# Five changes of order in a two-block transformer kernel: where a residual is scaled, when weight strips are split, when rows are turned, and how heads end

## The chip, the cores and the metric

The kernel runs on one core of one Trainium2 chip. Times are device microseconds (us) of one execution. The kernel before takes 3137.26 us, the median of 3 runs (3134.35 to 3138.42). The core has a matrix engine (TensorE, PE in the profile, its weight loads PEld), three engines for elementwise work (VectorE is DVE, ScalarE is ACT, GpSimd is POOL), and a queue that issues the weight loads (SyncE, SP). The engines run their own instruction lists and wait for each other on semaphores.

## What is computed

The input is 512 tokens of 1024 features. Block 1 is a norm, a projection into a gated delta rule (4 heads) and a dilated window attention (4 heads of 128 in three groups), two gates and an output matrix. Block 2 has two layers, each of:

```python
x = x + 0.5 * swiglu(rms_norm_2(x, ffn1_norm[l]), ffn1_w_in[l], ffn1_w_out[l])
h = rms_norm_2(x, mix_norm[l])
z_mla, z_swa, z_na = jnp.split(h @ w_mix_in[l], [MLA_IN, MLA_IN + SWA_IN], axis=-1)
o = jnp.concatenate([rms_norm_2(o_mla, g[:MLA_OUT]), rms_norm_2(o_swa, ...), rms_norm_2(o_na, ...)], axis=-1)
x = x + o @ w_mix_out[l]
x = x + mem_xattn(rms_norm_2(x, mem_norm_x[l]), mem, mem_norm_m[l], ...)
x = x + 0.5 * swiglu(rms_norm_2(x, ffn2_norm[l]), ffn2_w_in[l], ffn2_w_out[l])
x = rms_norm_2(x, block_norm[l])
```

The mix has three attentions: latent attention (8 heads), windowed attention (4 heads of 64) and neighbourhood attention (4 heads of 64). The memory attention reads 256 memory tokens with 4 heads of 64. Every query and key head is normed (and some are rotated) before its scores. `swiglu` goes over 22 tiles of 128 hidden features.

## The kernel before

**Layout and precision.** Activations lie feature by token (`residual`, 8 tiles of 128x512). A matrix product in full precision is three matmuls: operands are split into a high part and a low part, and `halves_mm` (L378) issues high x high (L373), high x low and low x high (L374, L375). Weights come as strips of 128x1024 by DMA into a ring of four slots. ACT writes a strip's high part (`split_strip_act`, L358, cast at L361), DVE subtracts it from the strip and writes the low part (`split_strip_dve`, L364, L367). PE needs both, and there is room for two high parts, so the high part of strip s+2 waits until PE has finished strip s. A strip of 1024 columns is 24 matmuls on PE, each over 512 tokens.

**Feed-forward** (`ffn_pe` L405, `ffn_act` L473, `ffn_dve` L523). Per hidden tile PE multiplies two strips (gate, up). DVE scales each bank by the token's rstd (L536, L541), ACT takes the SiLU (L489), DVE multiplies (L547), ACT writes the product's high part (L494), DVE the low part (L549). Between these steps ACT and DVE split strips two ahead. The norm of the input is not applied in front of the matmuls: its sum over features is a matmul that `ffn_pe` issues after its third strip (`norm_pe`, L226), and rstd is used at the banks.

**Layer 2's first feed-forward.** The norm that ends layer 1 is folded into it. Squares are summed on GpSimd (L211, and the raw sum at L1766); PE sums both over the partitions (L226 and `raw_norm`, L1328); `folded_norm` on ACT (L1468) and DVE (L1615) makes a combined rstd out of the two in six short steps; then `normalise_residual` (L1625, instructions at L1627) scales the eight tiles of `residual` by layer 1's norm. `ffn_dve` calls it through `residual` after the first hidden tile.

**Jobs and units.** A *job* makes one pair of query or key heads or one head: matmuls of one strip, squares on ACT (L672), their sum over features on PE (L645, into a bank for sums), logarithm and exponential on ACT (L680, L683), gain or rstd on DVE (L710, L716), rotary steps on DVE (L733 to L738) and the product with the rstd (L748). A *unit* is 128 queries of one head: scores on PE (L833), bias and maximum on DVE (L962, L973), exponential on ACT (L903), turning on PE (L845), copy of the turned probabilities on ACT (L914), product with the values on PE (L859). Each engine has both as generators, and `take_turns` (L1013) runs them by one list of names that all three engines share: `mix_turns` (L1254) and `mem_turns` (L1260) in block 2, `sw_turns` (L2034) in block 1. A job j has two halves, "begin" (its matmuls and squares) and "finish" (the sum, rstd and products of job j-1). Normally begin j comes ahead of finish j-1; for numbers in `early` (`sums_first`, `sw_first`) finish comes ahead. Jobs that use split strips also split the strip two ahead, unless `split=False`.

**The mix's output** (L1376 to L1418). The eight feature tiles of the attention output are turned on PE (`rows_pe`); six inside the turns, the last two (which wait for the group norm's scaling, L1693) behind them; ACT and DVE write their halves (L1707 for the low one). `mix_out(n, ks)` (L1394) multiplies blocks ks of output tile n. Tiles 0 and 1 are multiplied first for blocks 0 to 5, then the memory's norm matmul and rows 6 and 7, then blocks 6 and 7 of both. DVE then scales the memory's eight tiles (L1721) ahead of the first residual addition (L1731) and the splits of strips 2 and on.

## Time and profile before

| | before |
|---|---|
| median of 3 runs | 3137.26 us (3134.35 to 3138.42) |
| the profiled execution | 3127.07 us |
| its span | 3125.2 us |
| PE busy | 2948.3 us (94%), 13424 matmuls |
| DVE, ACT, POOL busy | 1466.8, 1087.2, 237.8 us |
| mean granted clock of PE | 0.972 |
| share of PE in the chain that ended last | 65% |
| bytes read from memory | 234.51 MB, 76 GB/s over the span |

The profile is one execution, recorded instruction by instruction. A busy share says how much of the span an engine executed; a list of waits says for whom an engine stood idle just before an instruction; a timeline gives start and duration of each instruction or of a run of like ones, and in brackets the idle time before it with the instruction that ended it. The granted clock is the share of full speed that the chip's throttle gave to PE. A matmul's shown duration reaches to its modelled end and overlaps the next: consecutive matmuls start 0.23 us apart at full clock.

### The profile page before, as it was taken

What the parts mean: (1) busy time and instruction counts of PE and PEld (TensorE: products, weight loads), DVE (VectorE), ACT (ScalarE), POOL (GpSimd) and SP (SyncE); (2) the same over time, 40 slices, a digit from 0 to 9 for tenths busy, and PEclk for the clock granted to TensorE, in tenths of its full rate; (3) what the DMA queues carried; (4) which work ended last, traced back from release to release, by engine and by line L of the source; (5) the groups of instructions that cost most, each with busy time, mean ns of one, the idle gap of its engine ahead of it and who ended that gap; (6) DMA issues with size and microseconds to landing.
All of it is one profiled execution on the core that took longest, in us unless ns stands there. A gap on an engine that the chain in (4) does not pass through costs nothing.

```text
span 3125.2 us, 36179 instructions
## 1 busy us (share of the span) xinstructions
PE 2948.3 (94%) x13424; PEld 2326.3 (74%) x13424; DVE 1466.8 (47%) x2032; ACT 1087.2 (35%) x1771; POOL 237.8 (8%) x176
## 2 busy tenths in 40 slices
PE   8878989989899999998999999899999998999998
PEld 5567767768778888566768888788886677778886
DVE  5653247744354433555444443444434645354432
ACT  4412233433233222555333222322223645432221
POOL 0000000000010012100220002100022000120012
PEclk9989899989999999999999999999999999999999
DMA  3100121103322233011212232222322110223232
GB/s 119 54 14 14 64 81 54 51 31 95 124 78 97 98 102 139 23 50 34 71 56 90 100 105 94 71 99 94 105 93 101 34 48 31 71 81 100 94 109 73
DMA packets 68361, 238.04 MB, mean 76 GB/s; under 512 B 10272, under 2 KB 12448, under 8 KB 67616
## 3 DMA queue, kind: packets, MB, share of 16 engines
q1 hardware_dynamic: 66240, 227.87, 21.8%
q10 hardware_dynamic: 2016, 8.77, 0.8%
q8 instruction: 66, 1.08, 0.1%
q14 instruction: 39, 0.32, 0.0%
HBM read 234.51 MB, written 2.10 MB: 76 GB/s over the span
## 4 chain that ended last, share of the span: by engine, by line
PE 65%; DVE 3%; ACT 3%; issue 1%; DMA 0%; POOLq 0%; DVEq 0%; POOL 0%; ACTq 0%; SPq 0%; PEldq 0%
PE bank L373 18%; PE bank L374 18%; PE bank L375 18%; PE bank L859 2%; PE bank L833 2%; PE bank L635 2%; PE bank L845 1%; PE bank L645 1%; PE bank L1448 1%; ACT L_probs L903 1%; PE bank L1425 0%; DVE L_scores L951 0%; ACT L_w_hi L361 0%; DVE L_weight_ring_low L367 0%; PE bank L226 0%
## 5 line engine op out<-in xcount | busy, mean ns | idle before, releaser
L373 PE MATMUL bank<-L_h_hi,L_w_hi 128*128 128x512 f32 x1776 | 709.5, 400 | 32.1 <-DVE L_weight_ring_low L367 14.0
L374 PE MATMUL bank<-L_h_lo,L_w_hi 128*128 128x512 f32 x1776 | 695.0, 391 | 0.0
L375 PE MATMUL bank<-L_h_hi,L_weight_ring_low 128*128 128x512 f32 x1776 | 694.5, 391 | 0.0
L361 ACT CAST L_w_hi<-L_weight_ring 128x1024 fp32r<-128x1024 f32 (+2 forms) x292 | 325.7, 1115 | 923.0 <-PE bank L375 911.1
L367 DVE TENSOR_TENSOR L_weight_ring_low<-L_weight_ring,L_w_hi 128x1024 fp32r<-128x1024 f32 (+2 forms) x292 | 395.3, 1354 | 376.2 <-ACT L_w_hi L361 375.9
L373 PEld LDWEIGHTS bank<-L_h_hi,L_w_hi 128*128 128x128 f32 x1776 | 335.4, 189 | 116.4 <-issue 16.8
L374 PEld LDWEIGHTS bank<-L_h_lo,L_w_hi 128*128 128x128 f32 x1776 | 335.9, 189 | 74.7 <-issue 6.8
L375 PEld LDWEIGHTS bank<-L_h_hi,L_weight_ring_low 128*128 128x128 f32 x1776 | 335.7, 189 | 70.7
L373 PE MATMUL bank<-L_act_hi,L_w_hi 128*128 128x512 f32 x704 | 273.9, 389 | 0.0
L374 PE MATMUL bank<-L_act_lo,L_w_hi 128*128 128x512 f32 x704 | 273.9, 389 | 0.0
L375 PE MATMUL bank<-L_act_hi,L_weight_ring_low 128*128 128x512 f32 x704 | 273.9, 389 | 0.0
L373 PE MATMUL bank<-B_h_hi,B_w_hi 128*128 128x512 f32 x480 | 196.1, 409 | 4.9 <-ACT B_arena L2438 3.4
L211 POOL TENSOR_TENSOR L_squares_sum<-residual 128x512 f32<-128x512 f32 x9 | 11.2, 1243 | 2486.3 <-DVE residual L572 1008.5
L375 PE MATMUL bank<-B_h_hi,B_weight_ring_low 128*128 128x512 f32 x480 | 188.1, 392 | 0.0
L374 PE MATMUL bank<-h_low,B_w_hi 128*128 128x512 f32 x480 | 188.0, 392 | 0.0
L541 DVE TENSOR_TENSOR L_up<-bank,L_rstd 128x512 f32<-128x512 f32 x88 | 60.8, 690 | 243.8 <-PE bank L375 243.8
L859 PEld LDWEIGHTS bank<-L_area,L_probsT 128*128 128x128 f32 x960 | 131.5, 193 | 57.1 <-issue 25.6
L367 DVE TENSOR_TENSOR B_weight_ring_low<-B_weight_ring,B_w_hi 128x1024 fp32r<-128x1024 f32 (+1 forms) x94 | 106.4, 1133 | 142.9 <-ACT B_w_hi L361 140.4
L375 PEld LDWEIGHTS bank<-L_act_hi,L_weight_ring_low 128*128 128x128 f32 x704 | 132.2, 188 | 27.6
L374 PEld LDWEIGHTS bank<-L_act_lo,L_w_hi 128*128 128x128 f32 x704 | 132.2, 188 | 27.4
L373 PEld LDWEIGHTS bank<-L_act_hi,L_w_hi 128*128 128x128 f32 x704 | 132.2, 188 | 27.3
L361 ACT CAST B_w_hi<-B_weight_ring 128x1024 fp32r<-128x1024 f32 (+1 forms) x94 | 91.4, 974 | 154.7 <-PE bank L375 152.5
(304 smaller groups left out, 3901.6 us busy)
## 6 DMA issues: line engine op xcount, KB each, us to landing
L_weight_ring<-ffn_in SPq DMA_DIRECT2D x176, 512.0 KB, 3.2
L_weight_ring<-ffn_out SPq DMA_DIRECT2D x64, 704.0 KB, 4.0
B_weight_ring<-w_sqk SPq DMA_DIRECT2D x24, 512.0 KB, 3.2
B_weight_ring<-w_dn SPq DMA_DIRECT2D x16, 512.0 KB, 3.3
B_weight_ring<-w_gate SPq DMA_DIRECT2D x16, 512.0 KB, 3.2
L_weight_ring<-w_sna_qk SPq DMA_DIRECT2D x16, 512.0 KB, 3.2
L_weight_ring<-w_mix_out SPq DMA_DIRECT2D x16, 512.0 KB, 3.2
B_weight_ring<-w_sv SPq DMA_DIRECT2D x12, 512.0 KB, 3.3
```

The lines of the kernel that those rows point to most:

```text
L361: e.copy(hv.high(at)[:, 0:width], sh.ring[:, at % RING, 0:width]).then_inc(hv.w_hi_done, 1)
L367: e.tensor_tensor(hv.low(at)[:, 0:width], sh.ring[:, at % RING, 0:width], hv.high(at)[:, 0:width].bitcast(F32), ALU.subtract).then_inc(hv. ...
L373: e.matmul(out, a_hi, b_hi, start=start, stop=False)
L374: e.matmul(out, a_hi, b_lo, start=False, stop=False)
L375: return e.matmul(out, a_lo, b_hi, start=False, stop=stop)
L541: e.tensor_tensor(hv.up[:, :], sh.banks[2 * j + 1][:, :], sh.rstd[:, :], ALU.mult)\
L635: mm = e.matmul(bank[r0:r0 + rn, 0:job["width"]], w[:, off:off + rn], rhs, start=(i == 0 and m == 0), stop=(i == len(job["parts"]) - 1 and ...
L645: e.matmul(banks[sum_banks[b % len(sum_banks)]][:, 0:width], ones[0:kn, :], jb.sq[0:kn, b, 0:width], start=True, stop=True).then_inc(jb.su ...
L833: e.matmul(banks[b][:, 0:nk], q, k, start=True, stop=True).then_inc(at_.scored, 1)
L845: mm = e.transpose(banks[b][:, i * P:(i + 1) * P], at_.p[:, u % 2, kt * P:(kt + 1) * P], ident[:, :])
L859: mm = e.matmul(banks[at_.ob[ob]][:, c0:c0 + unit["dv"]], at_.pt[:, u % 2, i * P:(i + 1) * P], v, start=(i == 0), stop=(i == len(vs) - 1))
L903: e.activation(at_.p[:, u % 2, 0:nk], src, ACT.Exp, bias=at_.nm[:, s:s + 1], accum_out=at_.sums[:, s:s + 1]).then_inc(at_.exped, 1)
```

## The change

No instruction is added or removed on any engine; what changes is the order.

- `ffn_pe`: where a second norm matmul is wanted (layer 2's first feed-forward alone), both come after the second strip and not after the third. `ffn_dve`: the residual is scaled after the second hidden tile and not after the first.
- `sw_turns` and `sw_first`, block 1: job 6 is also one in which finish comes ahead of begin, and in the last of the four heads the turns end with job, job, unit, unit in place of job, unit, job, unit.
- The splits that ride on the eight jobs of the windowed and neighbourhood heads (and the last two latent ones) are taken out of the jobs and put between the two units of ten turns of `mix_turns`.
- The mix's output: tile 0's blocks 0 to 5, then rows 6 and 7 are turned, then tile 1's blocks 0 to 3, then the memory's norm matmul, then the remaining blocks.
- `mem_turns`: four jobs, three units, the last job, the rest; job 3 has finish ahead of begin.

```diff
@@ -419,7 +419,7 @@
                 mm.then_inc(sh.strip_done, 1)
-                if first and j == 1 and part == 0:
+                if first and (j, part) == ((1, 0) if more_norm is None else (0, 1)):
                     norm_pe(e, seen, sh)
@@ -550,9 +550,9 @@
     tile(0, 0, W_IN, split=False)
+    tile(1, 1, W_IN)
     if residual is not None:
         residual()
-    tile(1, 1, W_IN)
     with seen.loop(e, FT // 2 - 2, ready=[(sh.strip_done, 4), (sh.silu_done, 2), (hv.w_hi_done, 4),
@@ -1174,15 +1174,15 @@
                                      ones=(ones, QK2), scale=1.0 / QK2, gain=scaled_qg[:, layer, 0:1], rope="own", cos_sin=cs2,
-                                     dest=(qk[:, tile, :], QK2), split=h == MLA_HEADS - 1,
+                                     dest=(qk[:, tile, :], QK2), split=False,
                                      **({"needs": (v_done, layer * (2 * TT + 2) + TT + 1)} if h == 0 else {})))
...
                                      rows=(0, NOPE), width=T, ones=(ones, QK2), scale=1.0 / QK2, gain=g("mlak"),
-                                     dest=(qk[:, tile + 1, :], QK2), split=h == MLA_HEADS - 1))
+                                     dest=(qk[:, tile + 1, :], QK2), split=False))
 
...
             mem_parts = [[(k * P, (mem_hi[k], mem_lo[k])) for k in range(KT)]]
-            pair = dict(rows=(0, P), ones=(ones64, P), scale=1.0 / DH)
+            pair = dict(split=False, rows=(0, P), ones=(ones64, P), scale=1.0 / DH)
 
@@ -1195,9 +1195,10 @@
             mem_jobs = [dict(pair, parts=k_parts(1, KT, P, m_n, NMEM), width=NMEM, gain=g("memk"),
-                             dest=(qk[:, 2 * i + 1, :], P), split=i == 0) for i in range(2)]
+                             dest=(qk[:, 2 * i + 1, :], P)) for i in range(2)]
+            mem_jobs[0]["split"] = True
             mem_jobs[1]["needs"] = (v_done, (layer + 1) * (2 * TT + 2))
-            mem_jobs += [q_job(i, scaled_qg[:, layer, 3:4], mem_parts, number=jobs_before + len(mix_jobs) + 3 + i, split=False) for i in range(2)]
+            mem_jobs += [q_job(i, scaled_qg[:, layer, 3:4], mem_parts, number=jobs_before + len(mix_jobs) + 3 + i) for i in range(2)]
             mem_jobs[2]["needs"] = (sh.h_done, layer * H_PER + 3 * KT)
@@ -1253,11 +1254,12 @@
         for i in range(20):
-            mix_turns += ["unit", "unit"] + {17: ["norm"], 18: ["norm_used"]}.get(i, []) + ["job"]
+            mix_turns += ["unit"] + ["split"] * (i >= 10) + ["unit"] + {17: ["norm"], 18: ["norm_used"]}.get(i, []) + ["job"]
         mix_turns += ["unit", "unit", "row"] * 4
...
         mix_turns += ["unit"] * 2 + ["row"] + ["unit"] * 6
-        mem_turns = ["job"] * 5 + ["unit"] * (1 + 4 * TT)
+        mem_turns = ["job"] * 4 + ["unit"] * 3 + ["job"] + ["unit"] * (4 * TT - 2)
+        mem_first = (3,)
 
@@ -1400,16 +1402,18 @@
 
-                    for n in range(2):
-                        e.wait_ge(sh.x_done, seen.free(sh.x_done))
-                        halves_here(e, seen, sh, hv, at + n, True)
-                        mix_out(n, range(6))
+                    e.wait_ge(sh.x_done, seen.free(sh.x_done))
+                    halves_here(e, seen, sh, hv, at, True)
+                    mix_out(0, range(6))
+                    next(rows)
+                    next(rows)
+                    e.wait_ge(sh.x_done, seen.free(sh.x_done))
+                    halves_here(e, seen, sh, hv, at + 1, True)
+                    mix_out(1, range(4))
                     e.wait_ge(at_.o_done, 2 + 10 * layer + 8)
                     norm_pe(e, seen, sh, NMEM)
-                    next(rows)
-                    next(rows)
-                    for n in range(2):
-                        mix_out(n, range(6, KT))
+                    mix_out(0, range(6, KT))
+                    mix_out(1, range(4, KT))
                     for n in range(2, KT):
@@ -1429,7 +1433,7 @@
                     seen.ready(sh.h_done, KT)
-                    take_turns(mem_turns, job=jobs_pe_steps(e, seen, sh, jb, at, mem_jobs, hv, True),
+                    take_turns(mem_turns, job=jobs_pe_steps(e, seen, sh, jb, at, mem_jobs, hv, True, mem_first),
                                unit=attn_pe_steps(e, seen, sh, at_, mem_units, ident))
@@ -1546,6 +1550,11 @@
 
+                    def splits_act():
+                        for i in range(10):
+                            split_strip_act(e, seen, sh, hv, at0 + sna_at + i, KT * P)
+                            yield
+
                     def rows_act():
@@ -1561,7 +1570,7 @@
                     take_turns(mix_turns, job=jobs_act_steps(e, seen, sh, jb, mix_jobs, hv, at0 + sna_at - 2 * MLA_HEADS, sums_first),
-                               unit=attn_act_steps(e, seen, sh, at_, mix_units), norm=norms, row=rows)
+                               unit=attn_act_steps(e, seen, sh, at_, mix_units), norm=norms, row=rows, split=splits_act())
                     next(norms)
@@ -1579,7 +1588,7 @@
                     split_strip_act(e, seen, sh, hv, at0 + mem_q_at, KT * P)
-                    take_turns(mem_turns, job=jobs_act_steps(e, seen, sh, jb, mem_jobs, hv, at0 + mem_q_at - 1),
+                    take_turns(mem_turns, job=jobs_act_steps(e, seen, sh, jb, mem_jobs, hv, at0 + mem_q_at - 1, mem_first),
                                unit=attn_act_steps(e, seen, sh, at_, mem_units))
@@ -1695,6 +1704,11 @@
 
+                    def splits_dve():
+                        for i in range(10):
+                            split_strip_dve(e, seen, sh, hv, at0 + sna_at + i, KT * P)
+                            yield
+
                     def rows_dve():
@@ -1711,7 +1725,7 @@
                                unit=attn_dve_steps(e, seen, sh, at_, mix_units, stores("mix", o_tok, 8)),
-                               norm_used=scales, row=rows)
+                               norm_used=scales, row=rows, split=splits_dve())
                     next(scales)
@@ -1733,7 +1747,7 @@
                     seen.ready(sh.strip_done, 2)
-                    take_turns(mem_turns, job=jobs_dve_steps(e, seen, sh, jb, mem_jobs, hv, at0 + mem_q_at - 1, True),
+                    take_turns(mem_turns, job=jobs_dve_steps(e, seen, sh, jb, mem_jobs, hv, at0 + mem_q_at - 1, True, mem_first),
                                unit=attn_dve_steps(e, seen, sh, at_, mem_units, stores("mem", o_mem, 2)))
@@ -2032,8 +2046,9 @@
         sw_turns = ["job"] * 7 + ["unit"]
-        sw_turns += ["job", "job", "unit", "job", "job", "unit", "job", "unit", "job", "unit"] * (NH - 1) + ["unit"] * TT
-        sw_first = range(2 * len(sw_jobs) // NH, len(sw_jobs) + 1, len(sw_jobs) // NH)
+        sw_turns += ["job", "job", "unit", "job", "job", "unit", "job", "unit", "job", "unit"] * (NH - 2)
+        sw_turns += ["job", "job", "unit", "job", "job", "unit", "job", "job", "unit", "unit"] + ["unit"] * TT
+        sw_first = range(len(sw_jobs) // NH, len(sw_jobs) + 1, len(sw_jobs) // NH)
 
```

How this moves instructions, at three places. Behind a row's engine line stand the operation, the outputs and the inputs with the names of the program, and the shape.

DVE, layer 2's first feed-forward, from the norm's last step (L1622, in the changed kernel L1631) on, before:

```order
L1622 TENSOR_TENSOR L_rstd<-L_area 128x512
L536 TENSOR_TENSOR L_unsplit<-bank,L_rstd 128x512
L541 TENSOR_TENSOR L_up<-bank,L_rstd 128x512
L547 TENSOR_TENSOR L_unsplit<-L_up,L_unsplit 128x512
L549 TENSOR_TENSOR L_act_lo<-L_unsplit,L_act_hi 128x512
L1627 SCALAR_TENSOR_TENSOR residual<-residual,L_gains,L_area 128x512 x8
L536 TENSOR_TENSOR L_unsplit<-bank,L_rstd 128x512
L367 TENSOR_TENSOR L_weight_ring_low<-L_weight_ring,L_w_hi 128x1024
L541 TENSOR_TENSOR L_up<-bank,L_rstd 128x512
L367 TENSOR_TENSOR L_weight_ring_low<-L_weight_ring,L_w_hi 128x1024
L547 TENSOR_TENSOR L_unsplit<-L_up,L_unsplit 128x512
L549 TENSOR_TENSOR L_act_lo<-L_unsplit,L_act_hi 128x512
```

and after:

```order
L1631 TENSOR_TENSOR L_rstd<-L_area 128x512
L536 TENSOR_TENSOR L_unsplit<-bank,L_rstd 128x512
L541 TENSOR_TENSOR L_up<-bank,L_rstd 128x512
L547 TENSOR_TENSOR L_unsplit<-L_up,L_unsplit 128x512
L549 TENSOR_TENSOR L_act_lo<-L_unsplit,L_act_hi 128x512
L536 TENSOR_TENSOR L_unsplit<-bank,L_rstd 128x512
L367 TENSOR_TENSOR L_weight_ring_low<-L_weight_ring,L_w_hi 128x1024
L541 TENSOR_TENSOR L_up<-bank,L_rstd 128x512
L367 TENSOR_TENSOR L_weight_ring_low<-L_weight_ring,L_w_hi 128x1024
L547 TENSOR_TENSOR L_unsplit<-L_up,L_unsplit 128x512
L549 TENSOR_TENSOR L_act_lo<-L_unsplit,L_act_hi 128x512
L1636 SCALAR_TENSOR_TENSOR residual<-residual,L_gains,L_area 128x512 x8
```

The eight scalings of the residual move behind the four elementwise steps and two strip splits of the second tile.

DVE, the last head of block 1, the second-to-last job's product and what follows, before:

```order
L748 TENSOR_TENSOR B_arena<-B_gained,B_job_rstd 128x512
L962 TENSOR_TENSOR B_arena<-bank,B_arena 128x256
L962 TENSOR_TENSOR B_arena<-bank,B_arena 128x512 x2
L973 TENSOR_REDUCE B_neg_max<-B_arena 128x1
L733 TENSOR_TENSOR B_rope_tmp<-B_gained,B_arena 32x512
L734 TENSOR_TENSOR B_rope_tmp<-B_gained,B_arena 32x512
L736 TENSOR_TENSOR B_gained<-B_gained,B_arena 64x512
L738 TENSOR_TENSOR B_gained<-B_gained,B_rope_tmp 64x512
L748 TENSOR_TENSOR B_arena<-B_gained,B_job_rstd 128x512
```

and after:

```order
L748 TENSOR_TENSOR B_arena<-B_gained,B_job_rstd 128x512
L733 TENSOR_TENSOR B_rope_tmp<-B_gained,B_arena 32x512
L734 TENSOR_TENSOR B_rope_tmp<-B_gained,B_arena 32x512
L736 TENSOR_TENSOR B_gained<-B_gained,B_arena 64x512
L738 TENSOR_TENSOR B_gained<-B_gained,B_rope_tmp 64x512
L748 TENSOR_TENSOR B_arena<-B_gained,B_job_rstd 128x512
L962 TENSOR_TENSOR B_arena<-bank,B_arena 128x256
L962 TENSOR_TENSOR B_arena<-bank,B_arena 128x512 x2
L973 TENSOR_REDUCE B_neg_max<-B_arena 128x1
```

The rotary steps and the product of the last key move ahead of the three additions and the maximum of a unit.

ACT, one turn of the mix with the split in it, before (L361 casts the strip, L914 copies turned probabilities, L903 is a unit's exponential, L680 a job's logarithm):

```order
L672 ACTIVATE L_unsplit<-L_gained 128x512
L361 CAST L_w_hi<-L_weight_ring 128x1024
L914 COPY L_probsT<-bank 128x512
L903 ACTIVATE L_probs,L_row_sums<-L_scores,L_neg_max 128x256
L914 COPY L_probsT<-bank 128x512
L903 ACTIVATE L_probs,L_row_sums<-L_scores,L_neg_max 128x384
L680 ACTIVATE L_job_rstd<-bank 128x512
```

and after:

```order
L672 ACTIVATE L_unsplit<-L_gained 128x512
L914 COPY L_probsT<-bank 128x512
L903 ACTIVATE L_probs,L_row_sums<-L_scores,L_neg_max 128x256
L361 CAST L_w_hi<-L_weight_ring 128x1024
L914 COPY L_probsT<-bank 128x512
L903 ACTIVATE L_probs,L_row_sums<-L_scores,L_neg_max 128x384
L680 ACTIVATE L_job_rstd<-bank 128x512
```

The cast moves behind the first unit's copy and exponential; its low half on DVE moves in the same way behind a maximum.

## Rows read from the trace of the kernel before

**Rows 1.** The page's first part: engine, busy us (share of the span), instructions.

```profile
PE 2948.3 (94%) x13424; PEld 2326.3 (74%) x13424; DVE 1466.8 (47%) x2032; ACT 1087.2 (35%) x1771; POOL 237.8 (8%) x176
```

**Rows 2.** Waits of PE: line, waited for: us in total, times, longest.

```profile
PE bank L373 <- DVE L_weight_ring_low L367: 14.0, 4, 9.0
PE bank L833 <- DVE B_arena L748: 13.0, 4, 6.1
```

**Rows 3.** Timeline, layer 2's first feed-forward: start, duration, instruction, [idle before <-releaser].

```profile
1988.20 1.74 POOL L1766 TENSOR_TENSOR L_area<-L_area,L_squares 128x512 f32<-128x512 f32 x1
...
2009.78 5.38 DVE L1627 SCALAR_TENSOR_TENSOR residual<-residual,L_gains,L_area 128x512 f32<-128x512 f32 x8
...
2016.95 0.79 PE L373 MATMUL bank<-L_h_hi,L_w_hi 128*128 128x512 f32 x1 [9.04 <-DVE L_weight_ring_low L367]
```

**Rows 4.** Windows: us, busy of each engine (x), granted clock, DMA; and one wait.

```profile
1511.00:1515.00 4.00, 3.73 (x10) 2.66 (x9) 3.89 (x10) 1.46 (x2) 0.00 (x0) 0.58 0.21 63
1646.00:1650.00 4.00, 3.45 (x15) 2.84 (x16) 3.31 (x5) 1.58 (x3) 0.00 (x0) 1.00 0.37 131
2016.90:2020.30 3.40, 3.35 (x8) 2.67 (x9) 2.71 (x4) 1.08 (x2) 0.00 (x0) 0.51 0.00 0
...
1646.55 0.50 PE L373 MATMUL bank<-L_h_hi,L_w_hi 128*128 128x512 f32 x1 [1.65 <-DVE L_weight_ring_low L367]
```

**Rows 5.** Timeline, end of head 0 in block 1.

```profile
457.66 1.02 PE L645 MATMUL bank<-B_job_squares,shared_consts 128*128 128x512 f32 x2
...
459.93 0.63 ACT L683 ACTIVATE B_job_rstd<-B_job_rstd 128x512 f32<-128x512 f32 x1
...
463.55 0.69 DVE L748 TENSOR_TENSOR B_arena<-B_gained,B_job_rstd 128x512 f32<-128x512 f32 x1
...
467.03 0.68 DVE L733 TENSOR_TENSOR B_rope_tmp<-B_gained,B_arena 32x512 f32<-32x512 f32 x1
...
470.64 1.65 PE L833 MATMUL bank<-B_arena 128*128 128x128 f32 x6 [5.61 <-DVE B_arena L748]
```

**Rows 6.** Timeline, end of the last head in block 1.

```profile
632.24 1.49 DVE L973 TENSOR_REDUCE B_neg_max<-B_arena 128x1 f32<-128x1280 f32 x1
...
633.76 1.36 ACT L903 ACTIVATE B_arena<-B_arena,B_neg_max 128x1280 f32<-128x1280 f32 x1 [4.96 <-DVE B_neg_max L973]
...
637.95 1.06 PE L845 MATMUL bank<-shared_consts,B_arena 128*128 128x128 f32 x4
```

**Rows 7.** Timeline, turns of the mix in layer 1.

```profile
1410.01 1.03 ACT L361 CAST L_w_hi<-L_weight_ring 128x1024 fp32r<-128x1024 f32 x1
...
1411.58 1.10 PE L859 MATMUL bank<-L_area,L_probsT 128*128 128x64 f32 x8 [0.22 <-ACT L_probsT L914]
...
1419.16 0.69 DVE L710 TENSOR_TENSOR L_gained<-bank,L_rstd 128x512 f32<-128x512 f32 x1 [1.26 <-PE bank L375]
...
1443.54 1.12 PE L859 MATMUL bank<-L_area,L_probsT 128*128 128x64 f32 x4 [2.42 <-ACT L_probsT L914]
```

**Rows 8.** Timeline, the mix's output in layer 1.

```profile
1502.24 1.14 DVE L1693 TENSOR_SCALAR L_area<-L_area,L_group_sums 128x256 f32<-128x256 f32 x4 [2.25 <-ACT L_group_sums L1546]
...
1510.23 0.50 PE L373 MATMUL bank<-L_h_hi,L_w_hi 128*128 128x512 f32 x1 [1.72 <-DVE L_h_lo L1707]
...
1511.53 3.26 DVE L1721 SCALAR_TENSOR_TENSOR L_area<-L_memT,L_gains,L_job_rstd 128x256 f32<-128x256 f32 x8
...
1516.57 0.50 PE L373 MATMUL bank<-L_h_hi,L_w_hi 128*128 128x512 f32 x1 [1.20 <-DVE residual L1731]
```

**Rows 9.** Timeline, the memory queries in layer 1.

```profile
1569.94 0.59 PE L645 MATMUL bank<-L_unsplit,shared_consts 128*128 128x256 f32 x2
...
1571.96 0.42 ACT L683 ACTIVATE L_job_rstd<-L_job_rstd 128x256 f32<-128x256 f32 x1
...
1578.86 1.10 PE L645 MATMUL bank<-L_unsplit,shared_consts 128*128 128x512 f32 x2 [1.98 <-ACT L_job_rstd L683]
...
1583.98 0.69 PE L845 MATMUL bank<-shared_consts,L_probs 128*128 128x128 f32 x2 [1.52 <-ACT L_probs L903]
```

## The prediction, made before the changed kernel was run

> **What bounds the kernel now.** I read the page first. TensorE (PE) is busy for 94% of the span [rows 1], so only what PE executes or waits for can move the end; the change removes no matmul, so its whole room is the 177 us in which PE stands idle and the stretches in which it runs at half clock. Then I read the list of PE's waits, which says on whom it waits: two groups matter here, a split weight strip that comes late (14.0 us in 4 waits, one of them 9.0) and a query or key head that comes late in the first block (13.0 us in 4 waits) [rows 2]. Then the timelines of PE, VectorE (DVE) and ScalarE (ACT) around each edit, to see what ended last there. Last, the windows for the granted clock. I worked each edit forward from its first moved instruction with the durations of the rows; all times of the changed kernel below are such estimates.
>
> **Residual scaling and its norm, layer 2's first feed-forward.** Today PE stops for 9.04 us on the low half of a weight strip [rows 3]. DVE could not write it: it ran the eight scalings of the residual (5.38 us) first. Behind this stands the fold of the norms, which starts only when PE has put its norm matmul after the third strip. The change puts that matmul one strip earlier; one strip is 24 matmuls of 0.23 us [rows 4], 5.4 us. GpSimd's sums end at 1989.94 [rows 3], five us before even the earlier place, so PE does not wait there. ACT and DVE then run the fold about 5.2 us earlier, the tile's last subtraction ends near 2004.6 (the scalings that follow it start at 2009.78 now), and DVE goes to tile 1 and not to the scalings: the late low half is there at 2006.5, while PE wants it at 2007.8. The stop is gone. What is late next: after tile 1 (near 2012.2) the scalings run until 2017.6, then come one scaling of a bank and the low half of strip 7, ready near 2019.5. PE wants it at 2018.3: a new stop of 1.2 us. The old stop was followed by a stretch at half clock: 8 matmuls took 3.35 us [rows 4] where 8 x 0.23 = 1.8 would do, 1.5 us lost. **9.04 + 1.5 - 1.2 = 9.3 us gained**; between 8 (clock drop stays) and 10.8 (no new stop).
>
> **Head ends of the first block.** At the end of head 0, PE waits 5.61 us for the last key [rows 5]. The sum of its squares now comes ahead of the next job's 24 matmuls. There is one bank for sums, so this sum must wait for ACT's exponential of the job before, which ends at 460.56 [rows 5], while PE is free at 458.7 [rows 5]: a new stop of 2.0 us, but it lies ahead of 5.4 us of matmuls that now cover the rest. DVE does not stand still: its product for the job before ends at 464.24, the last key's four rotary steps and its product take 3.55 us (467.03 to the release at 470.64 [rows 5]), so the key is there near 467.8. **Gain 470.6 - 467.8 = 2.8 us** (1.5 to 4.4). At the end of the last head the order on DVE is turned too: rotary steps first, then the three additions and the maximum (3.1 us) of the unit that was ahead. DVE has no gap there, so the maximum is ready near 637.3, not 633.73, its exponential of 1.36 us ends at 638.7 and PE's transposes, which began at 637.95, begin then [rows 6]. **Loss 0.8 us** (from a gain of 1 to a loss of 2). The stop of 6.1 us [rows 2] is thus moved and not removed.
>
> **Weight splits between units.** Before the change the copy of the turned probabilities queues on ACT behind a split of 1.03 us, and PE stands 0.22 us at one unit, 2.42 us at the one with the group norm [rows 7]. Now copy and exponential go first. The price: DVE's low half waits for ACT's high half, which comes after an exponential, and the next maximum queues behind it; the second unit's exponential, the job's rstd and its product come about 0.5 us later. DVE idles 1.26 us before it scales the next job's bank [rows 7], so that is covered in the plain turns. It isn't where the group norm sits on ACT: I get 2.7 us in place of the 2.42 and a smaller stop before it. Nor in the last turn, where no matmuls of a job cover it and 0.45 us is given back. **Gain 0.5 us in each layer, 1.0** (loss of 2 to gain of 4).
>
> **Output rows turned in front.** Today PE multiplies twelve blocks of tiles 0 and 1, turns rows 6 and 7, then waits 1.72 us for their halves, and later 1.20 us for the residual of tile 0 [rows 8]. DVE has scaled the rows at 1503.4. Now PE turns them at 1503.5, covers the halves with four blocks of tile 1, and the memory norm's matmul is done near 1508.1. Its rstd is ready near 1509.1 and not 1511.5; DVE's eight scalings of the memory (3.26 us [rows 8]) end at 1512.4, the low half and the residual take 1.9 more, and PE goes on at 1514.3, not 1516.57. **Gain 2.3 us in each layer, 4.6** (1.2 to 6). It ends in a stop of 1.7 to 2.0 us for the residual: the chain over DVE is what is left.
>
> **Memory queries.** Before: 1.98 us for an rstd, then 1.52 us for the first probabilities [rows 9]. Now the sum of job 2 goes ahead of job 3's matmuls and must wait for the rstd of job 1 (ACT's exponential ends 1572.38 [rows 9]), PE being free at 1570.5 [rows 9]: a new stop of 1.9 us. Job 3's matmuls then cover job 2; the first transposes start near 1580.8, not 1583.98. But the sum of job 3 now falls between units (0.9 us), and its two products (1.5 us) on DVE push the maxima behind them: PE stops again for about 1.9 us at the fifth unit, which starts at 1587.9 and not 1589.2. **Gain 1.2 us in each layer, 2.4** (loss of 3 to gain of 5).
>
> **The clock.** Five of the new stops of about 2 us (one at head 0, two at the output rows, two at the queries) stand between matmuls at full rate. The windows show both outcomes: after the 1.72 us stop the granted clock is 0.58 over 4 us, after one of 1.65 us near 1646 it stays 1.00 [rows 4]. I count half of five at 1.5 us, **3.8 us lost** (0 to 7.5).
>
> The Trainium skill (TensorE: Matmul & The Clock Gate, section "HAM oscillation — how this bites in real kernels") describes waits that put the array back to half rate, so that the work behind each starts cold. [...] The trace agrees at 1511 and does not at 1646.
>
> Weight loads move with the strips, no queue is passed by a new transfer, and nothing was late on a load at these places: nothing for them; if that cover went, each would show as a wait for a strip.
>
> **Sum:** 9.3 + 2.8 - 0.8 + 1.0 + 4.6 + 2.4 - 3.8 = 15.5 us. The profiled execution took 3127.07 us, its span 3125.2; it should become 3111.6. The median of the runs shown is 10.2 us above that execution, and I take the difference from it: 3137.26 - 15.5 = 3121.8 us. About 0.2%, 6.3 us, is what a measurement of this kernel can tell from no change.
>
> **Rivals.**
> - *Only the residual scaling pays* (0.15). The other places wait on chains of short steps over DVE and ACT, and a shorter stop shows up one step later; for it speaks that I find a new stop at each of them. Then 8 to 9 us: 3129.
> - *The half-clock stretches go as well* (0.12). The 2.42 us stop and the stops at the queries are each followed by one; if the shorter new ones are not, 3.8 comes back and some 4 more: 3113.
> - *The stop at the residual returns* (0.05). If DVE gets to strip 7's low half much later than 2019.5 (tile 1's last subtraction near 2016 and not 2012.2), the 9.3 shrink to 5 and with two parts failing the rest is near 5 us: 3132.
> - *Slower* (0.04): the splits between units. In 10 turns of each layer DVE waits for ACT's high half. It decides at the 1.26 us of slack [rows 7]: up to there the delay (0.5 by my working) costs nothing; at 2.4 us each turn would lose 1.1, 22 us in 20 turns, which eats the 15.5 and leaves +6.5: 3144. Against it: every step of that turn has a row, and they add up to 0.5.
>
> **How the numbers follow.** The forecast (gain of 10 to 21 us) has 0.64. The range must leave out no more than 2 in 10: it reaches from 3112 (the case with the clock) to 3130 (the case in which only the residual pays), which leaves out the last two rivals and the thin ends of the others. Faster by over 0.2%: 0.64 + 0.12 + most of 0.15 = 0.88; within 0.2%: 0.08; slower: 0.04.
>
> **What would show it.** In the changed profile PE's longest wait on a low half should fall from 9.0 to about 1.2 us, with the eight scalings after the second tile; PE's stop at head 0 should be two short ones of 2.0 and 0.9; the stop at the last head should stay at some 4 to 6 us; at the output rows the 1.72 us wait should be gone and the one for the residual be 1.7 to 2.0; at the queries there should be stops of 1.9, about 1.3 and 1.9. I am wrong if stops of the units with a split grow beyond those of today, if PE waits for the norm's sums at its earlier place, or if the gain lies elsewhere than in these places.

## The result and the profile after

The changed kernel takes 3103.3 us (median of 4 runs, 3097.82 to 3109.48), the kernel before 3136.8 (4 runs); ratio 0.9894, 95% interval 0.9875 to 0.9914. With the executions of the later comparisons (two of the changed kernel, all of the kernel before) it is 3105.1 us over 14 runs against 3134.9 over 87 (one further run, 10215 us at a clock of 0.458, is left out): 29.7 us less. The forecast was 15.5. The profiled executions, 3127.07 and 3097.82 us, differ by 29.3.

The page's first lines, and PE's waits (line, waited for: us in total, times, longest), of the changed kernel:

```profile
span 3095.9 us, 36179 instructions
...
PE 2931.8 (95%) x13424; PEld 2319.6 (75%) x13424; DVE 1465.2 (47%) x2032; ACT 1088.5 (35%) x1771; POOL 237.9 (8%) x176
```

```profile
PE bank L845 <- ACT L_probs L903: 18.6, 18, 1.8
...
PE bank L859 <- ACT L_probsT L914: 8.7, 6, 2.6
...
PE bank L845 <- ACT B_arena L903: 8.2, 3, 3.7
...
PE bank L373 <- DVE L_weight_ring_low L367: 5.5, 4, 1.7
...
PE bank L645 <- ACT L_job_rstd L683: 4.8, 4, 2.0
PE bank L645 <- ACT B_job_rstd L683: 4.0, 2, 2.0
...
PE bank L373 <- DVE residual L1745: 3.8, 2, 1.9
```

The 9.0 us of [rows 2] are gone, and no wait for a key (L748) is among the first. In their place stand waits of 2 us and the 3.65 us at the last head. PE's idle time fell by 12.8 us (span less busy time: 176.9 and 164.1) and its busy time by 16.5, with the same matmuls: more than half of the difference is matmuls that ran at a higher clock. Since PE's work is the same, this is the split to ask of every part of the change: what PE no longer stands for, and what it executes faster. The places of the forecast in the timeline after (start, duration, instruction, idle before it):

```profile
455.62 2.04 PE L645 MATMUL bank<-B_job_squares,shared_consts 128*128 128x512 f32 x2 [2.01 <-ACT B_job_rstd L683]
...
462.06 0.69 DVE L748 TENSOR_TENSOR B_arena<-B_gained,B_job_rstd 128x512 f32<-128x512 f32 x1
...
463.67 0.83 PE L833 MATMUL bank<-B_arena 128*128 128x128 f32 x6
...
618.47 1.10 PE L645 MATMUL bank<-B_job_squares,shared_consts 128*128 128x512 f32 x2 [2.01 <-ACT B_job_rstd L683]
...
630.18 1.12 PE L845 MATMUL bank<-shared_consts,B_arena 128*128 128x128 f32 x4 [3.65 <-ACT B_arena L903]
...
1433.88 0.66 PE L859 MATMUL bank<-L_area,L_probsT 128*128 128x64 f32 x4 [2.60 <-ACT L_probsT L914]
...
1493.97 1.09 PE L1386 MATMUL bank<-shared_consts,L_area 128*128 128x128 f32 x8 [0.31 <-DVE L_area L1702]
...
1504.27 0.50 PE L373 MATMUL bank<-L_h_hi,L_w_hi 128*128 128x512 f32 x1 [1.89 <-DVE residual L1745]
...
1560.20 1.10 PE L645 MATMUL bank<-L_unsplit,shared_consts 128*128 128x512 f32 x2 [1.98 <-ACT L_job_rstd L683]
...
1570.42 0.44 PE L845 MATMUL bank<-shared_consts,L_probs 128*128 128x128 f32 x2 [1.19 <-ACT L_probs L903]
...
1577.27 0.44 PE L845 MATMUL bank<-shared_consts,L_probs 128*128 128x128 f32 x2 [1.75 <-ACT L_probs L903]
...
2006.20 0.50 PE L373 MATMUL bank<-L_h_hi,L_w_hi 128*128 128x512 f32 x1 [0.54 <-DVE L_weight_ring_low L367]
```

Forecast and found: 2.0 and 2.01 at head 0, where the second stop of 0.9 did not come; 4 to 6 and 3.65 at the last head (seven later traces with both edits of the heads have 1.83 us at L833 there as well); 2.7 and 2.60 at the group norm; 1.7 to 2.0 and 1.89 at the residual; 1.9, 1.3, 1.9 and 1.98, 1.19, 1.75 at the queries; 1.2 and 0.54 at the low half. Six of nine are within 0.2 us, and the others lie at the places named.

**Stages.** To see what each place is worth I cut every trace at instructions that all kernels issue in the same order and take differences of their starts: the rows of L361 on ACT (casts of weight strips, and eight ACT_TABLE_LOAD rows that the profile puts on that line; counted from 0: "strip 253"), the scalings of a job's bank on DVE (counted from 0: "j40"), and the first block of the mix's output on PE ("m0", "m1" for layer 2). Strip 253 starts at 1995.30 before and 1982.17 after, strip 260 at 2046.10 and 2022.94, so this stage took 50.80 and 40.77 us. The table has the 20 traces of this study; a trace is left out of a row where it has fillers at the place or, as e8, e9 and e10, a half or a variant of the edit.

| stage | place as before | place changed | PE idle in it, mean, before and changed |
|---|---|---|---|
| head 0 (j0 to j7) | 51.6 to 52.4 in 8 traces | 47.3 to 48.0 in 12 | 5.6, 2.1 |
| last head (strip 61 to 62) | 55.9 to 58.0 in 8, mean 57.4 | both edits: 57.6 to 59.0 in 8, mean 58.6; head 0's alone: 55.3, 55.3, 55.4 | 15.8, 16.5; head 0's alone 15.9 |
| mix turns (j40 to m0, j68 to m1) | 18 stages: 14 at 123.3 to 123.6, two at 122.1 (both in the profile of before), two at 120.5 | 22 stages, 120.2 to 120.3 | 9.7, 9.2 |
| mix output (m0 to strip 186, m1 to 332) | 14: three at 34.4 to 34.5 (two in the profile of before), ten at 35.8 to 36.1, one 37.4 | 24: 31.6 to 31.7 in 23, one 33.2 | 4.4, 2.2 |
| queries (strips 186 to 192, 332 to 338) | 10 traces: layer 1 mean 94.4 (92.1 to 94.9), layer 2 94.3 (92.0 to 94.9) | 8 traces: layer 1 mean 93.1 (90.5 to 95.4), layer 2 94.5 (91.9 to 95.4) | 6.0, 6.9 |
| residual (strip 253 to 260) | 50.8 to 52.1 in 6 | 40.8 in 12 | 9.0, 0.5 |
| delta rule (strip 22 to 33), in no edit | 188.1 to 193.6 | | 22.3 to 23.3 |

By these means the parts are worth 4.2, -1.2, 2 x 2.8, 2 x 4.1, 1.0 and 10.3 us: 28.1 in all, against 29.7 in the medians. Between the first two profiles alone they come to 22.2; 5.1 us of their difference lay ahead of the first edited place. PE's idle time fell by 3.5 us at head 0, 0.5 a layer in the turns, 2.2 a layer at the output and 8.5 at the residual, and rose by 0.6 at the last head and 0.9 a layer at the queries: 15.0 us in all. The other 13.0 us of the 28.1 are the same matmuls at a higher clock, 4.6 of them in the turns. The stages with one value when changed and several when not are the finding: what varies there is the clock.

### The profile page after: what moved, and what is told of

Same layout as the page of the kernel before. It is cut to its first block, busy times and chain, and to the rows that moved or that the text cites. A ratio compares the mean times of both kernels' runs of the same rounds, so it can differ in the third digit from the quotient of the medians.

```text
span 3095.9 us, 36179 instructions
## 1 busy us (share of the span) xinstructions
PE 2931.8 (95%) x13424; PEld 2319.6 (75%) x13424; DVE 1465.2 (47%) x2032; ACT 1088.5 (35%) x1771; POOL 237.9 (8%) x176
## 4 chain that ended last, share of the span: by engine, by line
PE 65%; DVE 3%; ACT 3%; issue 1%; DMA 0%; DVEq 0%; POOLq 0%; POOL 0%; ACTq 0%; SPq 0%; PEldq 0%
PE bank L373 18%; PE bank L375 18%; PE bank L374 18%; PE bank L859 2%; PE bank L833 2%; PE bank L635 2%; PE bank L845 1%; PE bank L645 1%; PE bank L1452 1%; ACT L_probs L903 1%; PE bank L1429 0%; DVE L_scores L951 0%; DVE L_h_lo L468 0%; ACT L_squares L1544 0%; DVE L_weight_ring_low L367 0%
## 5 line engine op out<-in xcount | busy, mean ns | idle before, releaser
L361 ACT CAST L_w_hi<-L_weight_ring 128x1024 fp32r<-128x1024 f32 (+2 forms) x292 | 326.0, 1116 | 918.2 <-PE bank L375 906.0
L373 PEld LDWEIGHTS bank<-L_h_hi,L_w_hi 128*128 128x128 f32 x1776 | 334.7, 188 | 103.1 <-issue 16.2
L859 PEld LDWEIGHTS bank<-L_area,L_probsT 128*128 128x128 f32 x960 | 132.0, 193 | 52.1 <-issue 27.9
L361 ACT CAST B_w_hi<-B_weight_ring 128x1024 fp32r<-128x1024 f32 (+1 forms) x94 | 91.5, 974 | 152.1 <-PE bank L375 152.0
```

What stands on the lines that cost most here:

```text
L361: e.copy(hv.high(at)[:, 0:width], sh.ring[:, at % RING, 0:width]).then_inc(hv.w_hi_done, 1)
L373: e.matmul(out, a_hi, b_hi, start=start, stop=False)
L859: mm = e.matmul(banks[at_.ob[ob]][:, c0:c0 + unit["dv"]], at_.pt[:, u % 2, i * P:(i + 1) * P], v, start=(i == 0), stop=(i == len(vs) - 1))
```

## The experiments

Each kernel was timed against the kernel before in five rounds, in 4 to 11 executions.

**One part alone.** e1 (both edits of the feed-forward), e2 (`split=False` and `"split"` in the turns), e3 (the hunk with `mix_out`), and the whole again:

> Only the feed-forward part of the change (both norm matmuls after the second strip, residual scaled after the second tile). Theory P (each part is worth what its own place shows, whatever the rest does): the stretch from the last strip split before it to the third hidden tile, 50.8 us in the kernel before and 40.8 in the changed one, is 40.8 here; the time falls by 10 us against the kernel before, to a ratio of 0.9968. The stretches it does not touch are those of before within what two executions differ by. Theory K (the clock: the change also raises the granted clock in the delta rule and other stretches that it does not touch): the delta rule ahead of the heads is shorter as in the changed kernel (strip 22 to 43 of ACT's splits in 255.7 us and not 259.8) and the time falls by 15 or more.

> Only the splits between the units. Theory P: 1.6 us in each layer, 3.2 us in all, most of it at the five turns from the 1410s on, ratio 0.9990. The prediction's working: 0.5 in each layer, 1.0 us in all. Theory K: 8 us or more, the rest in stretches that are not touched. A loss would mean that the part only pays together with another one.

> Only the output rows turned in front. Theory P: from the first block of the mix's output to the first matmul released by the residual 15.0 us and not 17.8, 2.8 us in each layer, 5.7 us in all, ratio 0.9982. Prediction's working: 2.3 in each layer and a clock drop behind the new stop in half of the cases. Theory K: 10 us or more.

> The changed kernel again, unaltered, on one chip with its parts. The parts found in the traces add up to 21.7 us (10.1 residual, 3.6 - 0.8 head ends, 3.2 splits, 5.7 rows, 0 queries); the medians so far differ by 33.5. Theory P with chance in the clock: over more runs the difference comes down towards 22 to 26 and the unchanged stretches scatter between executions of the same kernel. Theory K: it stays at 30 or more and the unchanged stretches are short in each of its traces.

Ratios 0.9971 (0.9958 to 0.9984), 0.9980 (0.9971 to 0.9989), 0.9976 (0.9967 to 0.9985) and 0.9916 (0.9900 to 0.9932): 9.1, 6.3, 7.5 and 26 us. Theory K falls: the delta rule took 191.2, 188.2 and 193.6 us in the three and 191.2 in the changed kernel's second trace; its clock scatters, whatever the kernel. But theory P falls short for the splits, where twice its 3.2 us came, just outside the interval; the rows' 5.7 us lie inside theirs, and there it is the stages (2 x 4.1 in the mean) that say more. The reason shows where e1's trace and that of before differ at places that e1 does not edit. The turns of the mix, windows of both (us, busy of PE, PEld, DVE, ACT, POOL, granted clock, DMA), before and then e1:

```profile
1444.00:1446.00 2.00, 2.00 (x7) 1.23 (x6) 1.93 (x8) 0.77 (x3) 0.00 (x0) 0.50 0.00 0
1446.00:1448.00 2.00, 2.00 (x8) 1.42 (x7) 1.43 (x4) 1.97 (x6) 0.00 (x0) 0.80 0.00 0
1448.00:1450.00 2.00, 2.00 (x11) 1.63 (x10) 1.50 (x2) 0.14 (x1) 0.00 (x0) 1.00 0.00 0
```

```profile
1449.00:1451.00 2.00, 2.00 (x7) 1.45 (x7) 1.93 (x8) 0.55 (x2) 0.00 (x0) 0.50 0.00 0
1451.00:1453.00 2.00, 2.00 (x5) 1.23 (x4) 1.65 (x5) 1.97 (x8) 0.00 (x0) 0.50 0.00 0
1453.00:1455.00 2.00, 2.00 (x6) 1.52 (x6) 1.50 (x2) 0.35 (x1) 0.00 (x0) 0.50 0.00 0
```

Both follow the same stop (2.42 and 2.41 us at L859). The half rate (1.2 GHz) lasted some 3.4 us in the one and 6.8 in the other, and the stage 122.1 and 123.6 us, with PE idle for 9.7 us in both. And the mix's output in e1, its wait for the residual and two windows around it:

```profile
1523.26 0.62 PE L373 MATMUL bank<-L_h_hi,L_w_hi 128*128 128x512 f32 x1 [2.75 <-DVE residual L1731]
```

```profile
1520.00:1522.00 2.00, 0.50 (x3) 0.07 (x1) 2.00 (x5) 1.25 (x2) 0.00 (x0) 1.00 0.80 268
...
1524.00:1526.00 2.00, 2.00 (x6) 1.51 (x6) 2.00 (x3) 0.00 (x0) 1.23 (x1) 0.50 0.06 23
```

In the profile of before the wait was 1.20 us [rows 8], with the clock at 0.58 ahead of it [rows 4]: DVE's chain set the end, so the slow matmuls cost nothing and only filled the wait. In e1 the clock held up to the wait of 2.75 us and fell behind it, where dense matmuls paid 1.6 us. The same stop and the same chain, at two prices.

**The other parts alone, and the whole with other queries.** e5 has the edits of `sw_turns` and `sw_first`, e6 those of `mem_turns` and `mem_first`, e7 all but these last, e8:

```diff
-        mem_first = (3,)
+        mem_first = ()
```

> Only the head ends of block 1. By the stages of the traces: head 0 (its first to the eighth scaling of a bank on DVE) 47.3 to 48.0 us in the changed kernel, 51.6 to 52.4 without the edit: 3.6 to 5 gained; the last head 0.8 lost. Theory P: ratio 0.9989, some 3.5 us. Theory K (clock raised everywhere): more than 6. The prediction's working: 2.8 - 0.8 and up to 1.5 for the clock behind the new stop, 0.5 to 2.

> Only the memory queries. Theory Q (the new stop of 1.98 us stands between dense matmuls, a half-clock stretch of 2.0 us follows it in each layer and eats the gain): 0.8 us gained in layer 1 and as much lost in layer 2, ratio within 0.9995 to 1.0005. Prediction's working: 1.2 us gained in each layer, less 1.5 for half of the four new stops, 2.4 - 3 = about 0. Rival: without the other parts the clock stays full there and the full 2.4 us are gained, ratio 0.9992.

> The changed kernel with the memory queries of before. Theory Q: the queries' stage is 94.5 to 94.9 us in both layers (in the changed kernel 93.7 and 95.4), and the time is that of the changed kernel within 1 us: ratio to before 0.9914 to 0.992. Rival (full gain of the queries' part hidden by chance): 2.4 us slower than the changed kernel.

> The changed kernel, with the last memory job behind three units as in the change, but the sum of job 2 behind job 3's matmuls as before (no job early). Theory Q: the stop of 1.98 us ahead of job 3's matmuls and its half-clock stretch (2.0 us) are gone, 4.0 us; in their place PE stands for the rstd and the product of job 2, and a first unit's exponential, some 3.0 + 1.2 us behind them, less the 1.2 of today: a loss of 0 to 1 against the changed kernel in each layer when the clock falls there too, a gain of 1 when it does not. If the half-clock stretch comes whatever stands ahead of it, each layer loses about 2.

Ratios 0.9995 (0.9986 to 1.0004), 1.0003 (0.9994 to 1.0012), 0.9903 (0.9887 to 0.9918) and 0.9919 (0.9906 to 0.9933). The heads gain 4 us at head 0 (52 to 48.0) and give back 1.5 at the last. The queries alone took 95.39 and 95.30 us: no gain, and not the 0.8 that theory Q had for layer 1 either. e7 came out at 94.69 and 92.03; five rounds do not tell it from the changed kernel. The stage shows why. With the edit PE is idle for 6.9 us a layer and not 6.0, since its three stops (1.98, 1.19, 1.75) are longer than the old ones (1.98, 0.43, 1.52); and both orders come to 92 us in some executions (91.9 to 92.1 in five stages with the edit, 92.0 and 92.1 in two without) and to 93.4 to 95.4 in others, by the clock. One stage with the edit, 90.5, lies below. In e8 the sum's stop is gone, but PE waits 3.5 us in each layer for the query head (L745), and the stages are 95.87 and 95.48. The window behind the stop at 1560.20 in the changed kernel:

```profile
1562.00:1564.00 2.00, 2.00 (x6) 1.55 (x5) 1.28 (x2) 0.60 (x1) 0.00 (x0) 0.50 0.00 0
```

**The feed-forward's halves, and stops that are filled.** e9 has only the condition with `more_norm`, e10 only `residual()` behind `tile(1, 1, W_IN)`. e11 is the kernel before with fillers at the output rows, e12 the changed kernel with them ahead of the queries' stop:

```diff
+                    def fill(bank, n):
+                        for _ in range(n):
+                            e.matmul(banks[bank][:, :], ones, hv.h_hi[:, 0, :].bitcast(F32), start=True, stop=True)
...
+                    fill(2, 2)
                     for n in range(2):
                         mix_out(n, range(6, KT))
                     for n in range(2, KT):
+                        if n == 2:
+                            fill(2, 1)
```

> One half of the feed-forward part on the kernel before: both norm matmuls after the second strip, the residual still scaled after the first hidden tile. By the prediction's working the fold ends 5.2 us earlier and with it the eight scalings and the late low half: the stop of 9.04 us becomes 3.8, the half-clock stretch stays, stage (strip split 253 to 260) 45.6 us in place of 50.8; ratio 0.9983. Rival: the stop is set by something else than the norm and stays.

> The other half: the residual scaled after the second hidden tile, the norm matmuls after the third strip as before. The low half that PE waits for then comes 5.4 us earlier, so the stop of 9.04 becomes 3.7; the scalings end near 2022.8 and the low half of strip 7 near 2024.7, for which PE, that went on at 2011.6, waits from 2022 on: a second stop of 2.6. Stage 47 to 48 us, ratio 0.999. If both halves are worth 5 each, neither is worth 10 alone and the whole is 40.8.

> The kernel before with its stops at the mix's output filled: two matmuls into a bank that nobody reads stand in the 1.72 us wait for the low halves, one in the 1.20 us wait for the residual, in both layers. They take no wait away and leave nothing out. Theory H (in seven of ten untouched traces of this place a half-clock stretch of 1.6 us follows the stops, because PE stood still): stage m0 to strip 186 is 34.5 us in both layers with granted clock 1.00, and the median falls by 2 to 3 us, ratio 0.9992. Rival (the clock falls there for a reason that has nothing to do with the stops): 36.05 us in most cases, or longer by what the fillers take, ratio 1.000 to 1.001.

> The changed kernel with the new stop of 1.98 us at the memory queries filled by two such matmuls in each layer. Theory H: the half-clock stretch of 2.0 us behind it goes, the stage of the queries is 91.8 to 92.5 us in layer 1 and 92.5 to 93.5 in layer 2 (changed kernel: 93.7 and 95.4), 3 to 4 us in all, ratio to before 0.990. Rival (the clock falls anyway): no gain, stages 93.7 to 95.5.

e9 and e10: 0.9971 (0.9959 to 0.9983) and 0.9974 (0.9965 to 0.9984). What is left of the stop is what the expectations say, and the stages are 46.41 and 46.38 us: 4.4 gained by each half, 10.0 by both. The 1.2 over the sum fits the half rate behind the stop, which goes only with both (the first matmul behind it lasts 0.80 us in either half, 0.50 in the changed kernel). e10's second stop did not come. PE's wait in e9, then in e10:

```profile
2018.53 0.80 PE L373 MATMUL bank<-L_h_hi,L_w_hi 128*128 128x512 f32 x1 [3.69 <-DVE L_weight_ring_low L367]
```

```profile
2017.65 0.80 PE L373 MATMUL bank<-L_h_hi,L_w_hi 128*128 128x512 f32 x1 [3.74 <-DVE L_weight_ring_low L367]
```

Their medians fell by some 9 us each, more than the stage: their layer 2 turns took 120.5 us each, by a clock that nothing in them explains. e11, 0.9984 (0.9974 to 0.9995), decided nothing: the first wait was filled, but PE then still stood 1.91 us for the residual, the clock fell behind that, and the stages stayed at 36.06 and 36.09. Behind the wait for the residual is also where it fell in most traces without fillers (11 of 14 stages). The 5 us by which e11 was faster stand in no stage; its profiled execution, 3135.65 us, was the slowest of its eleven. e12, 0.9906 (0.9892 to 0.9921), against 0.9916 and 0.9902 of the changed kernel: the clock held where it had been 0.50, and layer 1 took 92.8 us, but layer 2 94.7, both above the ranges expected (91.8 to 92.5, 92.5 to 93.5). The fillers stood behind the wait for job 2's squares, so PE was still idle for 1.16 us ahead of them, and they delayed the sum: from the sum of job 1 to that of job 2 it took 3.57 us, where it is 2.57 unfilled (e13). The window behind the filled stop in e12:

```profile
1571.00:1573.00 2.00, 2.00 (x9) 1.36 (x8) 0.00 (x0) 1.21 (x2) 0.00 (x0) 1.00 0.00 0
```

**The whole, its last head, its splits.** e13 is the changed kernel, e14 has before's turns for the last head (head 0 keeps its edit), e15 also before's queries, e16 is the change without the splits:

```diff
-        sw_turns += [...] * (NH - 2)
-        sw_turns += ["job", "job", "unit", "job", "job", "unit", "job", "job", "unit", "unit"] + ["unit"] * TT
+        sw_turns += ["job", "job", "unit", "job", "job", "unit", "job", "unit", "job", "unit"] * (NH - 1) + ["unit"] * TT
```

> The changed kernel once more, as the neighbour of the next three on one chip. By the stages of the traces so far a part is worth: residual 10.0, splits 3.3 in each layer, rows 4.4 in each layer, head 0 4.4, last head -0.8, queries about 0: 28 us against the kernel before, ratio 0.9910. Theory K: 33 as in the first comparison, ratio 0.9894.

> The changed kernel with the turns of block 1's last head as before (job 6 still has finish ahead of begin). The prediction's working put a loss of 0.8 us on that edit; the stage from strip split 61 to 62 is 57.6 us in the changed kernel and 56.8 in the kernel before. Theory P: 56.8 here, the time 0.8 us below the changed kernel (less than five rounds can tell, the stage can). Rival: the exchange of job and unit is needed with head 0's edit, and the stage stays or grows.

> The changed kernel without its two parts that earned nothing: memory queries and last head as before. Theory P: the queries' stage 94.6 us in layer 1 and 92.0 to 94.8 in layer 2, the last head 56.8; 0.8 to 3 us below the changed kernel, ratio to before 0.9902 to 0.9908. Rival: the queries' edit gains something that the stages do not show, and the time is 1 to 2 us above.

> The changed kernel with the splits inside the jobs as before. Theory H (a half-clock stretch follows the stop at the group norm in either order; it lasted 6.8 us in most traces with the splits inside the jobs and 3.4 with the splits between the units): the stages j40 to m0 and j68 to m1 are 123.5 us again in most cases, 6.5 us in all above the changed kernel. By the waits alone (the prediction's way) it would be 3.8 in all by the aligned traces and 1.0 by my working.

Ratios 0.9902 (0.9887 to 0.9916), 0.9893 (0.9878 to 0.9908), 0.9894 (0.9879 to 0.9909) and 0.9917 (0.9903 to 0.9931). Without the splits the turns took 123.57 and 123.49 us against 120.2 in e13, 6.6 in all as theory H says. Behind the stop at the group norm PE ran at half rate for 6.8 us in both; over all traces with the splits in the jobs that is 6.8 us in 11 stages, 3.4 in 5 and none in 2, and with the splits between the units 3.4 in all 22. The time was 4.2 us longer; my own size, 0.5 a layer, is out as the worth of the edit. e15, with before's queries, came 2.8 us above e14 in the medians and 1.2 above e18 below, too little to tell. The last head is where the study found something to mend: 58.9 us in e13, 55.3 in e14, not the 0.8 of my working. But of these 3.6 us the waits make 0.8 (PE idle 16.7 and 15.9); the rest is again the clock. And e14's turns and waits at this head are those of the kernel before, whose stage took 57.4 in the mean: why it ran faster behind head 0's edit is open. The two windows of half rate in e13's last head:

```profile
642.00:644.00 2.00, 2.00 (x11) 2.00 (x10) 0.00 (x0) 0.00 (x0) 0.00 (x0) 0.50 0.03 8
654.00:656.00 2.00, 2.00 (x6) 1.04 (x7) 0.00 (x0) 0.59 (x1) 0.00 (x0) 0.56 0.00 0
```

**The longest stop filled.** e17 is e14 with six matmuls ahead of the wait for the last key, e18 is e14 again:

```diff
+            if h == NH - 1:
+                def fill(e):
+                    e.wait_ge(jb.gained, 2 + 6 * NH - 1)
+                    for _ in range(6):
+                        e.matmul(banks[0][:, :], ones, sh.h_hi[:, 0, :].bitcast(F32), start=True, stop=True)
+                sw_units[-TT]["fill"] = fill
```

> The kernel of e14 (the change with the last head's turns as before), with the stop of 6.13 us for the last key filled: six matmuls into a bank that nobody reads stand ahead of that wait, nothing is left out. Theory H (a long stop brings PE to half clock, and what it does behind the stop is charged for it; where it lands decides the cost): the granted clock stays near 1.00 at the last head, the waits stay, and the stage from strip split 61 to 62 falls from 55.3 us to 52 to 54, the time by 1.5 to 3. Rival (the half-clock stretches there are not a matter of standing still, or are hidden behind waits for ACT): 55.3 us or more.

> The kernel of e14 unaltered, as the neighbour of e17 and as a second look at the version that beat the changed kernel by 5.8 us in the medians of five runs. By the stages (55.3 us at the last head, 58.9 in the changed kernel) 3.6 us are real: ratio to before 0.9890 to 0.9895. If the 5.8 were chance, 0.9905.

Ratios 0.9894 (0.9876 to 0.9911) and 0.9898 (0.9883 to 0.9913). The two traces, e14 unfilled and then e17 filled. Timeline and windows of e14:

```profile
636.94 0.79 PE L833 MATMUL bank<-B_arena 128*128 128x128 f32 x2 [6.13 <-DVE B_arena L748]
...
653.93 0.66 PE L845 MATMUL bank<-shared_consts,B_arena 128*128 128x128 f32 x4 [2.08 <-ACT B_arena L903]
```

```profile
638.00:640.00 2.00, 1.70 (x8) 1.40 (x7) 0.42 (x2) 0.59 (x1) 0.00 (x0) 0.50 0.00 0
654.00:656.00 2.00, 2.00 (x11) 1.30 (x12) 0.52 (x1) 0.59 (x1) 0.00 (x0) 1.00 0.00 0
```

And of e17:

```profile
628.89 5.31 PE L2052 MATMUL bank<-B_h_hi,shared_consts 128*128 128x512 f32 x12
...
635.19 0.49 PE L835 MATMUL bank<-B_arena 128*128 128x128 f32 x2 [0.98 <-DVE B_arena L748]
...
650.25 0.65 PE L847 MATMUL bank<-shared_consts,B_arena 128*128 128x128 f32 x4 [2.08 <-ACT B_arena L905]
```

```profile
636.00:638.00 2.00, 1.22 (x10) 0.84 (x8) 0.61 (x3) 1.05 (x2) 0.00 (x0) 1.00 0.00 0
652.00:654.00 2.00, 2.00 (x7) 1.45 (x6) 0.69 (x1) 0.59 (x1) 0.00 (x0) 0.50 0.00 0
```

With the stop filled the half rate behind it is gone, and the next transposes come 15.06 us after L833 began, not 16.99: 1.9 us won. In the eleven traces with this stop unfilled it is 16.2 to 18.2. So here standing still is what brings the half rate, as far as one filled execution can show it. But then the next stop, 2.08 us in both, was followed by half rate in e17 and by full rate in e14, and the stage ended at 55.6 against 55.3 us, outside the 52 to 54 expected. Half rate behind this second stop is not new: seven of the eight traces with the heads of the kernel before have it too. Whether the filler brought it is not shown. e18 repeats e14's stage (55.4), and its ratio lies between the two expected; its nine executions with e14's have a median of 3099.5 us, 5.7 below the changed kernel's, of which the stage shows 3.2 in the mean. The intervals against the kernel before overlap, so the medians alone do not show it; the stage, 55.3 to 55.4 in three traces and 57.6 to 59.0 in eight, does.

## Why the prediction was wrong

The direction was right, the size was not: 3103.3 us, or 3105.1 over all runs, lies below the range's end of 3112. The gain was 14.2 us above the forecast's 15.5. By the means of the stages 4.6 of these are the splits, 3.6 the output rows, 1.4 head 0, 1.0 the residual, 3.8 the charge for the clock, which the stages already contain; the last head takes 0.4 off and the queries 1.4; 1.6 stand in no stage.

- **Waits.** The working of the stops held: six of the nine named were found within 0.2 us. **Residual**: 9.3 forecast, 10.0 found. The new stop is 0.54 and not 1.2: counted by the clock of the trace before (13.1 us later), PE asks for the low half at 2018.8 and not 2018.3, and it is there at 2019.3 and not 2019.5. The 2018.3 was a slip: two strips of 24 matmuls at 0.227 us behind 2007.8 end at 2018.7. **Last key**: ready at 462.75, where the forecast's 467.8 lies by the shift of 5.1 us between the traces; and the stage shows 4.2, not 2.8. PE stood 3.6 us less (5.61 against 2.01), because the second stop of 0.9 was missing: the half rate behind the first made PE so late that the key was there. In e4's trace the clock held and the second stop came, with 0.62 us (468.64, the line below); the stage was 47.3, only 0.7 shorter than the 48.0 of the others. So the half rate cost 0.7 there. **Output rows**: 2.3 a layer forecast, 2.8 between the two profiles and 4.1 in the mean; PE's idle time gives 2.2 of it.

```profile
468.64 0.94 PE L833 MATMUL bank<-B_arena 128*128 128x128 f32 x6 [0.62 <-DVE B_arena L748]
```

- **The clock.** This step failed, by what it left out. It had the clock cost 2.3 us net (3.8 lost at the new stops, 1.5 won behind the residual's old one); the stages show 13.0 us won. The charge itself was not far off. With the excess of the dense matmuls' spacing over 0.23 us, 2.0 us lay behind head 0's stop in ten of twelve traces, 2.0 or a little less behind the 1.98 us stop of the queries in ten of sixteen stages, 1.6 behind that at the residual in one of 24 (at the first two 0.4 to 0.5 us of it stand also where the clock held). But only the residual scaling was credited with the stretch behind its old stop. The old stops at the group norm and at the rows had such stretches too, longer or dearer in most executions than in the one I read, and they shrank (mostly 6.8 us to 3.4 in the turns) or went (the rows): 2.3 us a layer at the turns and 1.9 at the rows. The rival "the half-clock stretches go as well" (0.12, 3113; its own terms give 3114) named that term, some 4 us of it. But its condition did not come true: the new stops at head 0 and the queries were followed by half rate in most cases, and the one at the group norm always, so its 3.8 us did not come back. No rival had the size. The Trainium skill (TensorE: Matmul & The Clock Gate, section "HAM oscillation — how this bites in real kernels") tells of waits for DMA behind which the work starts at half rate; e17 agrees, in that with the 6.13 us stop the half rate behind it was gone. The stops of 1.9 to 2.1 us here, shorter than the waits on that page, were followed by either rate.
- **Splits.** 0.5 a layer forecast, 1.9 between the profiles, 2.8 in the mean of all (0.3 of each is DVE's j40, which itself starts later against PE). As a sum of waits the 0.5 was right: 0.22, 0.33 and 0.66 us went, the big one grew to 2.60, another came, and PE's idle time in the stage fell from 9.7 to 9.2. The rest is the clock behind the big stop.
- **The base.** I took the difference from the median, 10 us above the profiled execution, without asking what those 10 us were. Some 6 of them were the turns and rows of both layers, 1.4 to 1.6 us each, short in the profile of before and long in most others. They were part of the price of the old stops.
- **Last head.** 0.8 us lost forecast, and 1.2 found against the kernel before, but 3.2 against the same kernel with the old turns; the waits alone give 0.6 in both.
- **Queries.** 2.4 forecast before the clock's charge, 1.0 found with it. The forecast's own stops (1.98 and 1.52 before; 1.9, 1.3 and 1.9 after) add up to more than the old ones, and with the same work on PE that can't gain at an equal clock. The start at 1583.98 [rows 9], against which the 1.2 was counted, stands in a half-rate stretch of the trace of before (clock 0.50 from 1580 to 1586).

Open is what makes one stop of 2 us end at full rate and another, of the same length at the same place, at half rate; why the half rate in the turns always lasts 3.4 us with the splits between the units (120.2 us in 22 stages), while the stop there is no shorter; why the last head's stage is 2.1 us shorter behind head 0's edit; and the 1.6 us between the parts' sum and the medians.

## What to carry to other kernels

PE's work unchanged, an edit can gain what PE's idle time loses, and what the clock gives: add up the stops before and after for the first, and price the second by itself. Before costing an edit from one profile, compare that execution with the median of the runs: if it is faster, find in which stage, because a gain there is larger than its rows say. Count with an old stop also what runs slowly behind it, and where: half rate is free as long as another engine sets the end, and is paid in dense matmuls. And take an edit's parts apart even when the whole wins: without one of them, here, it ran 3.2 us shorter at its place.
